# One norm factor between two transformer blocks, keys and first queries projected by tiles, context prepared beside the feed-forward block

## The reference

```python
hx = modulate(rmsnorm(x, g_norm1[l]), mx[0], mx[1])
hc = modulate(rmsnorm(ctx, g_norm1[l]), mc[0], mc[1])
px = jnp.split(hx @ w_in[l], IN_SPLIT_IDX, axis=-1)
pc = jnp.split(hc @ w_in[l], IN_SPLIT_IDX, axis=-1)
...
qx = apply_rope(rmsnorm(heads(px[0], ATT_HEADS, ATT_HEAD_DIM), g_q[l]), cos, sin)
kx = apply_rope(rmsnorm(heads(px[1], ATT_KV_HEADS, ATT_HEAD_DIM), g_k[l]), cos, sin)
...
x = x + mx[2] * (jnp.concatenate([att_x, hg_x], axis=-1) @ w_out[l])
```

## Time and profile before

| | |
|---|---|
| median of 3 runs (lowest, highest) | 3335.62 us (3332.84, 3340.41) |
| profiled execution | 3333.01 us, its span 3331.2 us |
| PE busy, share of the span | 3100.7 us, 93% |
| DVE, ACT, POOL busy | 1553.6, 1002.6, 433.9 us |
| granted PE clock, mean | 0.973 of full speed |

### The profile page before, as it was taken

The page is one execution under the profiler, slowest core; times in us unless marked ns, Lnnn a source line. Parts: engine busy times, 40 slices in busy tenths (PEclk is TensorE's granted clock), DMA queues, the critical chain, the costliest instruction groups (busy, mean ns, idle before and its releaser), DMA issues. The chain is left out here.

```text
span 3331.2 us, 36380 instructions
## 1 busy us (share of the span) xinstructions
PE 3100.7 (93%) x15051; PEld 2518.8 (76%) x15051; DVE 1553.6 (47%) x1912; ACT 1002.6 (30%) x1440; POOL 433.9 (13%) x343
## 2 busy tenths in 40 slices
PE   7899999979999999999688998989879999999998
PEld 5788888867788888887565666877767788888886
DVE  7566656652664543333456761654463322222223
ACT  5555555542211111112423332222222211111111
POOL 4222223221000000001100000332131000000001
PEclk9999999999999999999888999999999999999999
DMA  3111111112233331112110001010012111111111
GB/s 124 33 45 45 45 45 45 45 64 102 89 108 120 114 97 49 50 46 87 42 51 5 9 10 41 20 38 32 26 58 100 42 47 50 46 51 45 51 43 59
DMA packets 77237, 184.78 MB, mean 55 GB/s; under 512 B 7056, under 2 KB 29072, under 8 KB 77072
## 3 DMA queue, kind: packets, MB, share of 16 engines
q1 hardware_dynamic: 77072, 182.44, 17.5%
HBM read 163.87 MB, written 15.79 MB: 54 GB/s over the span
## 5 line engine op out<-in xcount | busy, mean ns | idle before, releaser
L497 PE MATMUL ps<-b 128*128 128x512 f32 x5928 | 1474.4, 399 | 46.4 <-DVE b L1316 15.0
L497 PEld LDWEIGHTS ps<-b 128*128 128x128 f32 x5928 | 1091.3, 190 | 259.4 <-issue 26.8
L1512 PE MATMUL ps<-b 128*128 128x512 f32 x2592 | 608.5, 395 | 0.5 <-DVE b L1643 0.5
L1512 PEld LDWEIGHTS ps<-b 128*128 128x128 f32 x2592 | 485.1, 187 | 119.0 <-DVE b L1643 1.0
L486 DVE TENSOR_TENSOR b<-b 128x1024 fp32r<-128x1024 f32 (+1 forms) x206 | 254.7, 1237 | 326.9 <-ACT b L478 319.9
L2806 PE MATMUL ps<-b 128*128 128x512 f32 (+1 forms) x1584 | 363.9, 386 | 37.1 <-DVE b L1866 14.4
L478 ACT ACTIVATE b<-b 128x1024 fp32r<-128x1024 f32 (+1 forms) x206 | 215.1, 1045 | 562.7 <-PE ps L1512 463.8
L2806 PEld LDWEIGHTS ps<-b 128*128 128x128 f32 x1584 | 283.6, 197 | 94.8 <-issue 42.7
L1381 POOL TENSOR_TENSOR b<-b 128x1024 f32<-128x1024 f32 x24 | 57.5, 2397 | 1642.7 <-ACT b L1387 1642.3
L1558 ACT ACTIVATE b<-ps 128x1024 f32<-128x1024 f32 x54 | 55.4, 1025 | 389.2 <-PE ps L497 389.2
L2152 PE MATMUL ps<-b 128*128 128x512 f32 x320 | 163.0, 592 | 0.0
(11 more groups left out here) (291 smaller groups left out, 3297.1 us busy)
## 6 DMA issues: line engine op xcount, KB each, us to landing
b<-in_down SPq DMA_DIRECT2D x52, 512.0 KB, 3.6
b<-in_mod SPq DMA_DIRECT2D x96, 256.0 KB, 2.7
b<-in_gu SPq DMA_DIRECT2D x44, 512.0 KB, 3.6
b<-scratch SPq DMA_DIRECT2D x38, 512.0 KB, 4.4
b<-in_dn_in SPq DMA_DIRECT2D x32, 512.0 KB, 4.9
b<-in_up SPq DMA_DIRECT2D x32, 512.0 KB, 3.7
b<-in_win SPq DMA_DIRECT2D x26, 512.0 KB, 4.0
scratch<-b SPq DMA_DIRECT2D x18, 512.0 KB, 3.0
```

The costliest lines, as they stand in the source:

```text
L497: ins = e.matmul(ps[:, c], w, h[:, k, c], start=first and k == 0 and i == 0, stop=last and k == KT - 1 and i == 2)
L1512: ins = e.matmul(ps[:, c], w, u[:, at[k], c], start=k == 0 and p == 0, stop=k == n - 1 and p == 2)
```

## The change

- The first norm's factor and the second's are joined. ACT takes two squares of each of x1's tiles in the last down group, one weighted by `cw` (the root of norm_final squared plus 1e-6), one plain; POOL adds up both. The weighted sum gives one factor for both norms (`wfa` = norm_final times the modulation gain). x1 is no longer scaled in place: it is stored raw from the down group on, and the plain sum's factor (`st[:, 32:40]`) is applied when x1 comes back at w_out (8 scaled tiles on DVE, 8 transposes on PE).
- Between, PE takes each x tile as soon as it is ready, for the units win 4 and win 0 together (96 products); the context part of win 4 follows (24). DVE makes all low parts, over three buffers.
- The context's load, sums, factor and tiles are steps of `beside`, in the second half of the feed-forward block.
- The barriers at both ends of between are gone. The rope tables are loaded once the context's keys are taken out, and the fifth win unit's weights behind them on SP.
- Chains 0 and 1 start together; chain 2 follows 1, 3 follows 0, 4 follows 2. Unit win 1 waits for no chain, win 2 for chain 1, win 3 for chain 2, win 5 for chain 0.

The core of the diff:

```diff
 def attention_projections(side):
-    yield from side.project(("win", 4))
-    side.ready.add(0)
-    for m in range(4):
-        while side.stage < m - 1:
+    side.ready |= {0, 1}
+    for m, free in ((1, None), (2, 1), (3, 2)):
+        while free is not None and free not in side.done:
             yield "idle"
         yield from side.project(("win", m))
         side.ready.add(m + 1)
-    while side.stage < 4:
+    while 0 not in side.done:
         yield "idle"
     yield from side.to_tokens(("win", 5))
...
+        if name == "w_out":
+            rows(e, self.psl[3], self.st[:, 32:40], self.con("ident")).then_inc(*P.up("rf"))
...
+
+        P, A, V, G = sig
+        for c, w in ((0, self.cw[:, k:k + 1]), (1, 1.0)):
+            if k >= 2:
+                e.wait_ge(*G.at("acc", "d", k - 1, c))
+            e.activation(m["sq"][c] if k else m["accs"][c], m["x"][:, k, :], ACT.Square, scale=w).then_inc(*A.up("sq", "d", k, c))
...
+            if gate is not None:
+                e.wait_ge(*P.at("rf"))
+                e.scalar_tensor_tensor(out=x, in0=x, scalar=self.par("norm_final")[:, i:i + 1], in1=self.psl[3],
+                                       op0=ALU.mult, op1=ALU.mult).then_inc(*V.up("first", i))
+                e.wait_ge(*V.last())
...
+                    if gated:
+                        self.pe_stat(e, m, sig, "d")
+                    else:
+                        self.pe_stat2(e, m, sig, 0, self.psl[3]).then_inc(*P.up("cs", "d", KT - 1))
...
+        for k in range(KT):
+            e.dma_start(self.c_x[:, k, :], self.a["ctx"][:, k, :]).then_inc(*self.xl[k].up("ctx"))
...
+        e.wait_ge(*V.at("mt", 11))
+        e.wait_ge(*G.at("acc", "c", KT - 1))
+        col_sums(e, S, self.c_acc, self.con("ones"), True, True, 2).then_inc(*P.up("cs", "c"))
+        for _ in range(4):
+            yield
+        e.wait_ge(*V.at("rc", "c"))
+        rows(e, S[:, 512:768], self.st[:, 32:34], self.con("ident")).then_inc(*P.up("rw", "c"))
...
+        e.wait_ge(*V.at("ms", "c"))
+        e.activation(self.st[:, 34:36], self.st[:, 32:34], ACT.Sqrt).then_inc(*A.up("rt", "c"))
+        e.wait_ge(*V.at("cw"))
+        e.activation(self.cw, self.cw, ACT.Sqrt).then_inc(*A.up("cw"))
...
     def sp_between(self, e):
-        V = self.b2[2]
+        last = FF1 - 4
         for k in range(KT):
-            e.dma_start(self.c_x[:, k, :], self.a["ctx"][:, k, :]).then_inc(*self.xl[k].up("ctx"))
-        for k in range(KT):
-            e.wait_ge(*V.at("y", k))
+            e.wait_ge(*self.mm1[2].at("down", last, k))
             e.dma_start(self.scratch[1][:, k, :], self.x1[:, k, :]).then_inc(*self.xst.up(k))
-        self.sp_weights(e, UNIT["win", 4] + 5)
-        self.after_between(e)
...
     def pe_between(self, e):
         P, A, V, G = self.b2
-        ident, ones = self.con("ident"), self.con("ones")
-        e.wait_ge(*V.at("rc", "f"))
-        rows(e, self.psl[2], self.st[:, 0:8], ident).then_inc(*P.up("rw", "f"))
+        ident = self.con("ident")
+        j4, j0 = UNIT["win", 4], UNIT["win", 0]
+        e.wait_ge(*V.at("rc"))
+        rows(e, self.psl[2], self.st[:, 0:8], ident).then_inc(*P.up("rw"))
+        self.pe_stat2(e, self.m1, self.mm1, 1, self.psl[3]).then_inc(*P.up("cs", "f"))
         for k in range(KT):
-            e.wait_ge(*A.at("sq", "x", k))
-            col_sums(e, self.psl[3], self.c_sq[k % 2], ones, k == 0, k == KT - 1).then_inc(*P.up("cs", "x", k))
+            e.wait_ge(*V.at("l", k))
+            for i, j in enumerate((j4, j0)):
+                if k == 0:
+                    e.wait_ge(*self.ww.at(j))
+                for part in range(2):
+                    ins = self.gemm_piece(e, self.psl[i], j, k, part, self.b_hi, self.b_lo)
+                if k == KT - 1:
+                    ins.then_inc(*(self.gm.up(j) if i else P.up("keys")))
+        e.wait_ge(*self.mm1[2].at("l", "c", KT - 1))
         for k in range(KT):
-            e.wait_ge(*A.at("sq", "c", k))
-            col_sums(e, self.psl[1], self.c_sq[k % 2], ones, k == 0, k == KT - 1, 2).then_inc(*P.up("cs", "c", k))
-        e.wait_ge(*V.at("rc", "c"))
-        rows(e, self.psl[0], self.st[:, 16:18], ident).then_inc(*P.up("rw", "c"))
-        e.wait_ge(*V.at("rc", "x"))
-        rows(e, self.psl[2], self.st[:, 0:8], ident).then_inc(*P.up("rw", "x"))
+            hi, lo = blk(self.whi[j4 % SPL], k), blk(self.wlo[j4 % SPL], k)
+            for i, (w, x) in enumerate(((hi, self.c_hi), (hi, self.c_lo), (lo, self.c_hi))):
+                ins = e.matmul(self.psl[2][:, 0:TC], w, x[:, k, :], start=k == 0 and i == 0, stop=k == KT - 1 and i == 2)
+        ins.then_inc(*self.gm.up(j4))
+        e.wait_ge(*V.at("msf"))
...
     def act_between(self, e):
         P, A, V, G = self.b2
-        st = self.st
...
+        Q = self.aq[1]
+        k4, q0 = ("win", 4), ("win", 0)
+        e.wait_ge(*V.at("ms"))
+        e.activation(self.st[:, 8:16], self.st[:, 0:8], ACT.Sqrt).then_inc(*A.up("rt"))
         for k in range(KT):
-            e.wait_ge(*V.at("y", k))
-            if k >= 2:
-                e.wait_ge(*P.at("cs", "x", k - 2))
-            e.activation(self.c_sq[k % 2], self.x1[:, k, :], ACT.Square).then_inc(*A.up("sq", "x", k))
...
-        root("x", 8, 0)
-        for k in range(KT):
...
-        for k in range(KT):
-            z = self.c_sq[k % 2]
-            e.wait_ge(*V.at("z", "x", k))
-            if k % 2:
-                e.activation(z, z, ACT.Identity, bias=self.mod[:, k, 0:1]).then_inc(*A.up())
-                e.wait_ge(*A.last())
-                e.activation(self.b_hi[:, k, :], z, ACT.Copy).then_inc(*A.up("h", "x", k))
-            else:
-                e.activation(self.b_hi[:, k, :], z, ACT.Identity, bias=self.mod[:, k, 0:1]).then_inc(*A.up("h", "x", k))
-        self.act_weights(e, UNIT["win", 4] + 3)
...
+            e.wait_ge(*V.at("z", k))
+            e.activation(self.b_hi[:, k, :], self.n_z[k % 3], ACT.Identity, bias=self.mod[:, k, 0:1]).then_inc(*A.up("h", k))
+            if k == 2:
+                self.act_weights(e, UNIT[k4] + 3)
+        e.wait_ge(*P.at("keys"))
+        e.activation(self.z[0][:, TC:TA], self.psl[0], ACT.Copy).then_inc(*Q.up("ev", k4, 0))
+        e.wait_ge(*self.gm.at(UNIT[q0]))
+        e.activation(self.z[1], self.psl[1], ACT.Copy).then_inc(*Q.up("ev", q0, 0))
+        e.wait_ge(*self.gm.at(UNIT[k4]))
+        e.activation(self.z[0][:, 0:TC], self.psl[2][:, 0:TC], ACT.Copy).then_inc(*Q.up("ev", k4, 2))
+        e.wait_ge(*V.at("msf"))
+        e.activation(self.st[:, 40:48], self.st[:, 32:40], ACT.Sqrt).then_inc(*A.up("rtf"))
...
     def dve_between(self, e):
...
-        mean("f", self.psl[3], 8, 0)
-        e.wait_ge(*P.at("rw", "f"))
+        e.wait_ge(*self.mm1[0].at("cs", "d", KT - 1))
+        e.tensor_scalar(st[:, 0:8], self.psl[3][:, 0:1024:128], 1.0 / D, EPS * EPS, ALU.mult, ALU.add).then_inc(*V.up("ms"))
+        e.wait_ge(*A.at("rt"))
+        e.reciprocal(st[:, 0:8], st[:, 8:16]).then_inc(*V.up("rc"))
+        e.wait_ge(*P.at("rw"))
...
+        scaled(0)
...
-            x = self.x1[:, k, :]
-            e.scalar_tensor_tensor(out=x, in0=x, scalar=self.par("norm_final")[:, k:k + 1], in1=self.psl[2],
-                                   op0=ALU.mult, op1=ALU.mult).then_inc(*V.up("y", k))
-        e.wait_ge(*P.at("cs", "c", KT - 1))
-        mean("c", self.psl[1], 2, 16)
-        mean("x", self.psl[3], 8, 0)
...
-        for k in range(KT):
-            z = self.c_sq[k % 2]
-            if k >= 2:
-                e.wait_ge(*(G if k % 2 else V).at("l", "x", k - 2))
-            else:
-                e.wait_ge(*V.at("l", "c", KT - 2 + k))
-            e.scalar_tensor_tensor(out=z, in0=self.x1[:, k, :], scalar=self.ax[:, k:k + 1], in1=self.psl[2],
-                                   op0=ALU.mult, op1=ALU.mult).then_inc(*V.up("z", "x", k))
...
+            if k + 1 < KT:
+                scaled(k + 1)
+            e.wait_ge(*A.at("h", k))
+            e.scalar_tensor_tensor(out=self.b_lo[:, k, :], in0=self.n_z[k % 3], scalar=self.mod[:, k, 0:1],
+                                   in1=self.b_hi[:, k, :].bitcast(F32), op0=ALU.add,
+                                   op1=ALU.subtract).then_inc(*V.up("l", k))
+        e.wait_ge(*P.at("cs", "f"))
+        e.tensor_scalar(st[:, 32:40], self.psl[3][:, 0:1024:128], 1.0 / D, EPS, ALU.mult, ALU.add).then_inc(*V.up("msf"))
...
-    def pool_between(self, e):
-        P, A, V, G = self.b2
-        for k in range(1, KT, 2):
-            e.wait_ge(*A.at("h", "x", k))
-            e.tensor_tensor(self.b_lo[:, k, :], self.c_sq[k % 2], self.b_hi[:, k, :].bitcast(F32),
-                            ALU.subtract).then_inc(*G.up("l", "x", k))
...
+    CHAIN_Z = (0, 1, 2, 1, 2)
+    CHAIN_SLOT = (0, 1, 1, 0, 1)
+    CHAIN_BEHIND = (None, None, 1, 0, 2)
...
             for n in left[0:2]:
                 if next(chains[n], self) is self:
                     left.remove(n)
-                    side.stage = left[0] if left else 5
```

(5 more changed lines are left out.)

236 lines of the change are left out of this document (135 added, 101 removed).

## The result

The changed kernel takes 3281.85 us (median of 4 runs, 3279.44 to 3284.2), the kernel before 3335.76 beside it: a ratio of 0.9837, 95% interval 0.982 to 0.9854. The profiled execution is one of 3279.44 us with a span of 3277.5, to be set against 3333.01 and 3331.2. So 53.7 us of span are gone in the profile, where the steps gave 45.8.

The account below looks back on a forecast made before the run. PE was taken as the bound, busy 93% of the span. Attention 47.7 us earlier, less 0.9 (feed-forward block) and 1.0 (w_out), gave 45.8: 3289.8 us from the median, likeliest 3290, forecast 3283 to 3298 (0.66), range 3279 to 3304.

Parts of the forecast that it names:

- Up to the factor: Last down product to the norm's factor: no table load ahead of the root, wait 0.28 instead of 1.63, gain 1.35 us.
- The between part: Norm and first products: plain sums, then 96 products without a wait in 22.6 us, DVE not in the way.
- T: End of the 96 products, units win 4 and win 0 done: forecast at 1597.7, 55.7 us earlier than before.
- The wait on SP: Start of the chains: fifth win unit's weights queue behind the rope tables, landing at T+9.1; PE stands 4 us.
- The clock behind T: From T to the attention: PE's gaps lower the clock; costs 0 to 10 us, 5 taken.
- The chains' order: From T to the attention: tails end at T+32.6, T+51.9, T+60.2, T+78.8 and T+95.3; attention T+99.8 before clock loss.
- Elsewhere, the feed-forward block: First feed-forward block: the context's 2 sums and 2 rows on a full PE cost 0.9 us; its passes are hidden.
- Elsewhere, w_out: Start of w_out: 8 added PE transposes cost 1.0 us on the path; the 8 DVE passes are hidden.
- Rival 1: Between part and chains: clock stays down longer; in part 3300 us (chance 0.13), wholly about 3370 (chance 0.03).
- Rival 2: Down group: POOL falls behind beside DVE's weight splits, sums come 4.9 us late, 3295 us; chance 0.08.
- Rival 3: Chains: no clock loss and weights land early, the wait on SP 4 us smaller, 3281 us; chance 0.08.
- Rival 4: Chains: their own serial steps take up the gain, attention starts as if nothing had moved, 3336 us; chance 0.02.

Follow-up runs that it names:

- experiment 7: Changed kernel with an added exponential forcing the root's table reload, 3285.92 us; the same plus a wait for PE's last sums ahead of the root, 3278.64 us.
- experiment 4: Changed kernel with the next win weight tile asked for at the start of SP's part, ahead of the x1 stores: 3269.3 us, ratio to before 0.9792.
- experiment 6: Changed kernel with the first query's chain held back until the keys' chain is through: 3303.6 us, ratio 0.9887.
- experiment 5: Changed kernel with the keys' and first queries' products waiting for the last of eight normed tiles: 3297.54 us, ratio 0.9876.
- experiment 9: Changed kernel with both barriers of the kernel before put back: 3282.19 us.
- experiments 1 and 8: Experiment 1, and the changed kernel with the context's column sums, its row of factors and w_out's eight transposes done twice: 3280.2 us.
- experiment 1: Kernel before with only the feed-forward activation tiles shifted, 64 bytes in the first block and 128 in the second: 3318.75 us beside 3337.89, ratio 0.9942.

## Why the prediction was right, and where it was not

- **Up to the factor.** No load, waits of 0.28: right in size. Its reason was half of it: an earlier root left the table, but experiment 7 shows that a load would have been hidden too, once no barrier stands ahead of it. The Trainium skill (ScalarE: Activation LUTs, What ACT_TABLE_LOAD costs) would have a drain of about 1380 ns besides; experiment 7 measured 1.34 in all, so the rows were the right choice.
- **The between part.** 96 products unbroken, right. T came 27.7 after the mean and not 30.2. The row was priced at 1.94, from half clock, and took 1.09; T had 0.8 for half clock in the sums, which ran at full clock; and the products were priced at 0.235 us each from the down products of the earlier trace rows, whose tiles lie at a slow distance (192), and took 0.230. No run here undoes the joined factor or the context's move by itself; that they give the 58.2 us is read from the traces, where 64 sums, 10 rows and the context's passes are gone from the stretch.
- **The wait on SP.** Right in place, short in size: ACT had the tile at T+12.2, not T+9.1, and PE stood 7.4 us, not 4. SP issued it at T+5.2, not T+4.3, and it landed 7.0 later, not 4.9.
- **The clock behind T.** 5 was taken. The wait on SP alone cost 3.3 in clock (experiment 4). Behind the later pauses 18 products took 5.97 at 1620.87 (4.24 at 1590.41) and 12 took 4.24 at 1657.22, about 3 more in PE's time; how much of that is on the path was not measured. The prediction called clock rows of 0.5 beyond 10 us together behind T a sign of being wrong. By windows of 5 us some 20 us ran at 0.5 there, yet the attention came close to forecast. The sign was badly chosen: it also counts time in which PE stands, as from 1598 to 1602 and from 1690 on.
- **The chains' order.** Right: the five tails keep their forecast spacing within 1.1 us, and experiment 6 shows 25.7 us if the pair is split. Without the hand-over tile by tile 19.9 are lost (experiment 5), with the barriers under 1 up to the chains (experiment 9).
- **The middle as a whole.** That 48.7 stands beside a forecast of 47.7 is partly luck: T came 2.5 us earlier after the mean than forecast, and the attention 1.5 later after T.
- **Elsewhere, the feed-forward block.** This term failed: -0.9 stood for what measured +7.45 to the mean, although the first down add came 1.6 us later (905.3, 903.8; no cause was looked for). The added work does cost 0.6 to 0.7 (experiments 1 and 8). What outweighed it, 9.6 us (663.7 to 654.1 in experiment 1), is that 1536 down products became 6.67 ns shorter by where their tiles lie. The prediction took the spacing of products as a constant from the earlier trace rows, and did not compare addresses.
- **Elsewhere, w_out.** 1.0 forecast, 0.9 measured. Timeline, PE, to be read beside the earlier trace rows:

```profile
2440.96 1.04 PE L79 MATMUL ps<-b 128*128 128x128 f32 x8
2441.75 2.99 PE L1362 MATMUL ps<-b 128*128 128x512 f32 x12
...
2517.66 1.97 PE L79 MATMUL ps<-b 128*128 128x128 f32 x8 [3.06 <-DVE b L1649]
```

- Of the other 1.6 given back, clock explains what was lost: of the lead of 56.0 us at 2414, 1.6 went when ten products took 4.12 instead of 2.53, and 0.9 in the norm's row at 2517.66, 1.97 where it had 1.09. Behind it 1.5 came back up to the last norm and 0.4 went again. No run here ties any of this to the change.
- **The rivals.** Rival 1 (the clock stays down): no; 0.98, 0.88 and 0.87 in the three windows. Rival 2 (POOL late): no; the last sums of the down group end at 1559.98, 0.04 before the mean, and the plain sums behind wait for no accumulator. Rival 3 in part is what experiment 4 made: the weights land early, the clock still falls behind later pauses. Rival 4: no.

The result, 3281.85, lies 8 us below the forecast. In the profile it is 7.9: the placement's 9.6, 1.0 more in the middle and 0.3 less for the context's work, less 1.5 more given back at the end and 1.6 lost at the start. Without the placement 44.1 of the 53.7 us are left for the change, under the 45.8 forecast. The result stands within the stated range of 3279 to 3304, but below the 3283 to 3298 held likeliest and beside rival 3's 3281, and neither of rival 3's conditions was met: what took it there is a term that the prediction did not have.
